# Constant matmuls on TensorE while it waits for the tokens' inverse roots, at five boundaries of a four-layer kernel

## The chip, the cores and the metric

The kernel runs on one core of one Trainium2 chip. The metric is the device time of one execution in microseconds (us). The core has five engines that run their own instruction streams and meet through semaphores: TensorE (PE, matmul), VectorE (DVE), ScalarE (ACT), GpSimd (POOL) and SyncE (SP, which here issues the loads of the weights).

## The reference

The reference is two model blocks of two layers each, run one after the other on 256 tokens of width 1024, all in float32.

```python
def first_block(x, ...):                       # l = 0, 1
    h = rmsnorm(x, g_mix[l])
    q, k, v, gates = split(h @ w_in[l])
    x = x + (g_sb * stick_breaking(q, k, v) @ w_o_sb[l] + g_fx * forgetting(q, k, v) @ w_o_fox[l]) @ w_out[l]
    h = rmsnorm(x, g_ffn[l])
    x = x + (swiglu(h, ...) if l == 0 else moe_swiglu(h, w_router, w_gu_exp, w_dn_exp))

def second_block(x, c, ctx, ...):              # l = 0, 1; a context xc of 256 tokens runs beside x in l = 0
    h = modulate(rms_norm(x, g_pre_mix[l]), sh1, sc1)
    y = mLSTM branch, grouped attention branch, neighbourhood attention branch of h @ w_in[l]
    x = x + ga1 * rms_norm(merge_branches(y) @ w_out[l], g_post_mix[l])
    f = conv_ffn(modulate(rms_norm(x, g_pre_ffn[l]), sh2, sc2), w_up[l], conv_w[l], conv_b[l], w_down[l])
    x = x + ga2 * rms_norm(f, g_post_ffn[l])
```

A norm divides each token's row by the root of its mean square. So no projection that follows a norm can start before that token's root is known, and the root needs the whole of the row that the projection before has just finished.

## The kernel before

Every projection is a *segment*: a list of *units* of weights (128 x 1024 floats each) that SP loads, ACT rounds to an upper part (`w_hi`, line 1031) and DVE to the rest (`w_lo`, line 1542). PE multiplies each unit three times: upper weights by upper activations, upper weights by lower activations, lower weights by upper activations. A segment's results lie in PSUM, which has eight banks of 128 x 512 floats. Banks 0 to 3 hold the results of the projections (4 to 7 as well in a feed-forward segment), and steps beside them (attention, transposes) use banks 4 to 7.

The order of the work is that of a list, `plan`, made once; each engine walks the list in order. Where a norm stands between two segments, the plan has a `turn` step, and the segment behind it is started by `first_pair` on PE (lines 2575 to 2626). What happens at such a boundary:

- DVE (or ACT and DVE) finishes the residual sum `x_tm` from the last PSUM result.
- ACT squares each of the two tiles of 128 tokens with a running sum (line 1430), takes the root (line 1435); DVE takes the reciprocal (line 2215) and multiplies the identity by it (line 2216). That makes one diagonal matrix for each tile of tokens.
- PE multiplies 128 x 128 blocks of `x_tm` by these diagonals (`turn_item`, line 2571). So it transposes the tokens and divides by the root at once. Each item is two float32 matmuls, and each of these appears in the trace as two pieces. Four items go ahead, in banks 4 to 7; the first needs the first root for its first half, and the second root for its other half.
- ACT and DVE turn each item into `h_hi` and `h_lo`, with the gain only (lines 1455 and 2233) in the first block, with gain and shift (lines 1448, 1459, 2223, 2236) in the second. `first_pair` then multiplies two units of weights chunk by chunk (line 2616) as the items come, with one more `turn_item` behind each chunk.

PE has nothing to do between the last matmul of the old segment and the first `turn_item`. The boundaries that the change touches are five of the eight that go through `first_pair`:

| boundary | segment whose first pair follows | where in the code | about at (us) |
|---|---|---|---|
| A | first block, layer 1, stick-breaking q and k (`s_sb`) | `first_layer`, line 639 | 459 to 463 |
| B | first block, layer 1, router (8 columns) | `first_layer`, line 693 | 687 to 692 |
| C | second block, layer 0, feed-forward, 512 tokens | `second_layer`, line 859 | 1770 to 1775 |
| D | second block, layer 1, mLSTM q (`s_mq`) | `second_layer`, line 747 | 2199 to 2209 |
| E | second block, layer 1, feed-forward, 256 tokens | `second_layer`, line 859 | 2631 to 2638 |

At D the old segment ends with results for 512 tokens in banks 0 to 3. DVE adds the first two tiles (banks 0 and 1, line 1654) and raises `o_added`; the other two tiles are added later.

Of the kernel before, what the change touches and what calls it, by code (L numbers as in the profile page):

```python
# [16 lines left out]
TT = T // P  # L17
# [30 lines left out]
AHEAD = 2  # L48
# [67 lines left out]
class Segment:  # L116
# [4 lines left out]
    def __init__(self, units, iters, mode, at, evac, A=None, B=None, N=None, tiles=None, dst=None, scale=None, bias=None,  # L121
                 M=None, tmp=None, route=None, n_branch=None, gates=None, bias_layer=None, o=None, cw=None, cb=None,
                 down=None, ex=None, half=None, buf=None, mod_rows=None, mod_places=None, dt=0, after=0, gate0=None, y_pairs=0, y_turned=0,
                 ys=None, sums=False, spare=None):
        self.units, self.iters, self.n = units, iters, len(units)

        self.paced = mode in ("fm", "tm")
        self.uses, self.ride = [], {}
        self.dt, self.after, self.gate0, self.y_pairs, self.y_turned = dt, after, gate0, y_pairs, y_turned
        self.looped = iters > 2  # L130
        assert not self.looped or self.n % RAW == 0 and self.n % HL == 0 and all(u[0] >= 0 for u in units)
        self.results = max(u[0] for u in units) + 1
        self.next, self.first = None, False
        self.alone = mode == "moe"
        self.turned = {}
        self.sig = self.unit0 = self.result0 = self.flag = self.before = self.ready = self.x_at = None
        self.ringed, self.apart, self.clear = False, 0, None
        self.routes, self.routed = False, None
        self.split_at = [sum(u[0] >= 0 for u in units[:j]) for j in range(len(units) + 1)]
        self.splits, self.mods = self.split_at[-1], len(units) - self.split_at[-1]  # L140
        self.mod_rows, self.mod_places, self.mod0 = mod_rows, mod_places, None
        self.down = down if down is not None else self.results
        self.ex, self.half, self.buf = ex, half, buf
        self.mode, self.at, self.evac = mode, at, evac
        self.A, self.B, self.N, self.tiles = A, B, N, tiles
        self.dst, self.scale, self.bias, self.M = dst, scale, bias, M
        self.tmp, self.route, self.o, self.cw, self.cb = tmp, route, o, cw, cb
        self.n_branch, self.gates, self.bias_layer = n_branch, gates, bias_layer
        self.ys = ys
        self.sums, self.spare, self.tail, self.gains, self.turn, self.late, self.early = sums, spare, None, None, None, None, AHEAD  # L150
        self.down_at = next((j for j, u in enumerate(units) if mode == "ffn" and u[0] == FB), None)

    def parts(self, j):
# [59 lines left out]
def build(nc, a, out):  # L213
    ctx = ExitStack()
    with ctx:
# [18 lines left out]
        causal = sb("causal", [P, TT, T], F32R)  # L234
        anti = sb("anti", [P, TT, T], F32R)
        ident_r = sb("ident_r", [P, P], F32R)
# [218 lines left out]
        def tm_units(w, c0, q=0, chunks=DC, width=NT):  # L455

            n = UNIT // width
            return [(q, k, min(n, chunks - k), k == 0, k + n >= chunks, width,
                     lambda it, k=k: w[k * P:min(k + n, chunks) * P, c0:c0 + width].rearrange("(c p) n -> p c n", p=P))
                    for k in range(0, chunks, n)]  # L460
# [161 lines left out]
        def first_layer(l, before, ctx_turned):  # L622
# [13 lines left out]
            else:  # L636
                done = (main.results_saved, before.result0 + before.results * before.iters)
                turn_norm([0], lambda s: g_mix, None, 0, ready=[done] * TT, parts_first=True)
            s_sb = add_segment("fm", sum((fm_units(w, QK_SB + q * 2 * P, q) for q in range(4)), []), A=H, N=T, evac="fm", dst=qk,
                               scale=[HD ** -0.5] * 2 + [1.0] * 2)  # L640
            s_vsb = add_segment("tm", tm_units(w, V_SB), A=H, tiles=TT, evac="tm", dst=v_sb)
            if l == 0:
                spread(Step("prepare", dict(count), steps=2), units_of(s_vsb)[1:3])
# [43 lines left out]
            if l % 2:  # L687
# [5 lines left out]
                router = add_segment("fm", fm_units(a["w_router"][l // 2], 0, 0, N_EXP), A=H, N=T, evac="rows", dst=logits, bias=None,  # L693
                                     M=N_EXP)
                router.routes = True
                half, used, _ = router.uses[0][0]
                add("route", logits=logits, route=route, buf=buf, ready=(half_saved[half], used + 1), src=plan[-2])
                router_step = plan[-1]
# [12 lines left out]
            n = D_FF // FE  # L711
# [8 lines left out]
        def second_layer(l, before, ctx_turned):  # L720
# [12 lines left out]
            def span(t):  # L733
# [13 lines left out]
            s_mq = add_segment("fm", sum((fm_units(w, MQ + q * 2 * P, q) for q in range(2)), []), A=H, N=nq * P, evac="fm",  # L747
                               dst=mqk[:, 0:ML_H, :], scale=[1.0] * 2)
            if nq == TT:
                s_mq.late, s_mq.early = s_mq.turned["fresh"][0], AHEAD + 2  # L750
            s_mg = add_segment("fm", fm_units(w, MG, 0, 4 * ML_H), A=H, N=2 * T, evac="rows", dst=rows[0:4 * ML_H, 0, :],
                               bias=gate_bias[0:4 * ML_H, DEPTH + l:DEPTH + l + 1], M=4 * ML_H)
# [95 lines left out]
            for k in range(2):  # L848
# [12 lines left out]
                              evac="conv", tmp=view(FREE + 4096, 4, 2 * T), o=o, cw=col_second(l, "conv_w"),  # L861
                              cb=col_second(l, "conv_b"), down=FB, spare=view(3072, 2, 512))
            seg.tail = Step("tail", dict(count), rows=mod_rows if more else None, l=l + 1)
            seg.gains = gains(1, diag, nq // TT)
            n = FB * (D_FF // FE)
            seg.clear = mixed
# [1442 lines left out]
        def _(pe):  # L2309
# [265 lines left out]
            def first_pair(seg):  # L2575
# [3 lines left out]
                ah, al = seg.A  # L2579
                if not seg.paced:  # L2580
                    pe.wait_ge(seg.sig.results_saved, seg.result(0, 0))
                total = sum(seg.units[j][2] for j in range(2))
                sides = [o for o in order if (o[0] + 1) * T <= seg.N]
                for n, (s, base, own) in enumerate(sides):
# [286 lines left out]
```

## Time and profile before

| | |
|---|---|
| median of 3 runs | 2851.9 us (2850.53 to 2852.31) |
| the profiled execution's own time | 2847.78 us |
| its span, first to last instruction | 2846.0 us |
| PE busy | 2700.3 us, 95% |
| DVE busy, ACT busy | 59%, 48% |
| mean granted clock of TensorE | 0.984 of full speed |
| chain that ended last, by engine | PE 81%, ACT 7%, DVE 7%, issue 5% |

The granted clock is the share of full speed (2.4 GHz) that the chip lets TensorE have; in this profile it is 1.00 or 0.50 (1.2 GHz) at any one time. A mean between the two says for how much of a stretch it was down. A matmul's busy time includes its way through the array, so of matmuls in a row the distance from start to start is what each one costs.

### The profile page before, as it was taken

What the parts mean: (1) busy time and instruction counts of PE and PEld (TensorE: products, weight loads), DVE (VectorE), ACT (ScalarE), POOL (GpSimd) and SP (SyncE); (2) the same over time, 40 slices, a digit from 0 to 9 for tenths busy, and PEclk for the clock granted to TensorE, in tenths of its full rate; (3) what the DMA queues carried; (4) which work ended last, traced back from release to release, by engine and by line L of the source; (5) the groups of instructions that cost most, each with busy time, mean ns of one, the idle gap of its engine ahead of it and who ended that gap; (6) DMA issues with size and microseconds to landing.
All of it is one profiled execution on the core that took longest, in us unless ns stands there. A gap on an engine that the chain in (4) does not pass through costs nothing.

```text
span 2846.0 us, 40880 instructions
## 1 busy us (share of the span) xinstructions
PE 2700.3 (95%) x14980; PEld 2167.5 (76%) x14980; DVE 1677.7 (59%) x2555; ACT 1372.7 (48%) x2229; POOL 46.4 (2%) x58
## 2 busy tenths in 40 slices
PE   8999999998999999999999999999999899989998
PEld 7668888666888888677776677777777677667987
DVE  5654445655898998354545545553454456455766
ACT  5544345654776776333335344432333434445654
POOL 1000000000000000000000100000000010010000
PEclk9999999999999999899999999999999999999999
DMA  7437895434899997322231213364452234333464
GB/s 225 128 115 224 268 297 162 127 119 168 296 324 323 326 323 266 94 67 60 78 89 49 78 56 97 115 181 126 134 179 74 82 99 124 90 104 118 144 184 141
DMA packets 352458, 444.88 MB, mean 156 GB/s; under 512 B 19616, under 2 KB 197920, under 8 KB 352288
## 3 DMA queue, kind: packets, MB, share of 16 engines
q1 hardware_dynamic: 349792, 435.44, 48.7%
q0 software_dynamic: 2208, 6.79, 0.8%
q8 instruction: 109, 1.79, 0.3%
q14 instruction: 61, 0.50, 0.1%
q10 hardware_dynamic: 288, 0.36, 0.0%
HBM read 441.48 MB, written 1.05 MB: 155 GB/s over the span
## 4 chain that ended last, share of the span: by engine, by line
PE 81%; ACT 7%; DVE 7%; issue 5%; DMA 1%; SPq 0%; ACTq 0%; DVEq 0%
PE ps L2381 21%; PE ps L2409 16%; PE ps L2368 14%; PE ps L2422 8%; PE ps L2413 4%; ACT w_hi L1031 2%; PE ps L2430 2%; PE ps L2616 2%; PE ps L2731 2%; PE ps L2714 2%; PE ps L2571 1%; PE ps L2720 1%; PE ps L2447 1%; PE ps L2751 1%; DVE att L2081 1%
## 5 line engine op out<-in xcount | busy, mean ns | idle before, releaser
L1542 DVE TENSOR_TENSOR w_lo<-raw,w_hi 128x1024 fp32r<-128x1024 f32 (+1 forms) x578 | 684.9, 1200 | 529.8 <-ACT w_hi L1031 462.1
L1031 ACT ACTIVATE w_hi<-raw 128x1024 fp32r<-128x1024 f32 (+1 forms) x578 | 587.1, 1030 | 273.4 <-PE ps L2381 126.0
L2409 PE MATMUL ps<-w_hi,h_hi 128*128 128x512 f32 (+1 forms) x992 | 402.8, 408 | 11.5 <-DVE h_lo L1993 3.9
L2409 PE MATMUL ps<-w_hi,h_lo 128*128 128x512 f32 (+1 forms) x992 | 379.4, 385 | 0.0
L2368 PE MATMUL ps<-h_hi,w_hi 128*128 128x256 f32 (+1 forms) x1008 | 301.5, 324 | 15.5 <-ACT w_hi L1031 10.3
L2422 PE MATMUL ps<-w_lo,h_hi 128*128 128x512 f32 (+1 forms) x992 | 297.6, 384 | 0.0
L2368 PE MATMUL ps<-h_lo,w_hi 128*128 128x256 f32 (+1 forms) x1008 | 296.7, 320 | 0.0
L2368 PEld LDWEIGHTS ps<-h_hi,w_hi 128*128 128x128 f32 x1008 | 192.2, 191 | 49.4 <-ACT w_hi L1031 16.7
L2409 PEld LDWEIGHTS ps<-w_hi,h_hi 128*128 128x128 f32 x992 | 187.7, 189 | 48.4 <-issue 12.7
L2422 PEld LDWEIGHTS ps<-w_lo,h_hi 128*128 128x128 f32 x992 | 183.0, 188 | 39.5
L2381 PE MATMUL ps<-w_hi,act_hi 128*128 128x512 f32 x528 | 211.6, 401 | 0.0
L2409 PEld LDWEIGHTS ps<-w_hi,h_lo 128*128 128x128 f32 x992 | 187.4, 189 | 28.9 <-issue 1.0
L2381 PE MATMUL ps<-w_hi,act_lo 128*128 128x512 f32 x528 | 209.1, 396 | 0.0
L1542 DVE TENSOR_TENSOR w_lo<-arena,w_hi 128x1024 fp32r<-128x1024 f32 (+1 forms) x192 | 201.7, 1085 | 7.9 <-ACT w_hi L1031 7.4
L2368 PEld LDWEIGHTS ps<-h_lo,w_hi 128*128 128x128 f32 x1008 | 192.4, 191 | 12.8
L1369 ACT ACTIVATE arena<-ps,att 128x512 f32<-128x512 f32 (+2 forms) x128 | 72.7, 568 | 244.0 <-DVE att L2081 160.8
L1031 ACT ACTIVATE w_hi<-arena 128x1024 fp32r<-128x1024 f32 (+1 forms) x192 | 175.2, 947 | 24.2 <-PE ps L2381 23.6
L2368 PE MATMUL ps<-h_hi,w_lo 128*128 128x256 f32 (+1 forms) x1008 | 177.2, 318 | 0.0
L2368 PEld LDWEIGHTS ps<-h_hi,w_lo 128*128 128x128 f32 x1008 | 149.8, 191 | 13.1
L2381 PE MATMUL ps<-w_lo,act_hi 128*128 128x512 f32 x528 | 152.9, 400 | 0.0
L2381 PE MATMUL ps<-w_hi,h_hi 128*128 128x512 f32 (+1 forms) x384 | 145.7, 379 | 2.8 <-issue 2.8
L2381 PE MATMUL ps<-w_hi,h_lo 128*128 128x512 f32 (+1 forms) x384 | 142.8, 372 | 0.0
(301 smaller groups left out, 4214.3 us busy)
## 6 DMA issues: line engine op xcount, KB each, us to landing
raw<-in_w_in SPq DMA_DIRECT2D x196, 512.0 KB, 3.7
arena<-in_w_mod SPq DMA_DIRECT2D x96, 512.0 KB, 5.6
raw<-in_w_up SPq DMA_DIRECT2D x88, 512.0 KB, 4.7
raw<-in_w_gu_exp SPq DMA_DIRECT2D x64, 512.0 KB, 5.6
arena<-in_w_gu_exp SPq DMA_DIRECT2D x64, 512.0 KB, 4.8
arena<-in_w_gu_exp SPq DMA_DIRECT2D x64, 384.0 KB, 4.0
arena<-in_w_dn_exp SPq DMA_DIRECT2D x48, 512.0 KB, 6.4
raw<-in_w_gu_dense SPq DMA_DIRECT2D x44, 512.0 KB, 7.4
```

Of the source, the lines that this page charges most:

```text
L1031: nc.scalar.activation(w_hi[:, half, 0:n], place[:, 0:n], ACT.Copy).then_inc(seg.sig.hi_ready, 1)
L1369: nc.scalar.activation(prob[:, i0 % 2, 0:nk], z, ACT.Exp, bias=att[:, i0 % 2:i0 % 2 + 1], accum_out=att[:, 2 + i0 % 2:3 + i0 % 2]).then_in ...
L1542: nc.vector.tensor_tensor(w_lo[:, half, 0:n], place[:, 0:n], w_hi[:, half, 0:n].bitcast(F32), ALU.subtract).then_inc(seg.sig.lo_ready, 1)
L2368: ins = mm(dst, w[:, f0:f0 + wide], x[:, k + c, 0:seg.N], start=upper and k + c == 0 and x is ah, stop=not upper and k + c == DC - 1)
L2381: ins = mm(dst, x, w[:, c * width:(c + 1) * width], start=upper and opens and c == 0 and x is xh, stop=not upper and closes and c == m - 1)
L2409: ins = mm(ps[:, 2 * h + p % 2, 0:width], x[:, k + c, p * P:(p + 1) * P], wh[:, c * width:(c + 1) * width], start=opens and c == 0 and x i ...
L2413: ins = mm(ps[0:wide, 2 * h + p % 2, 0:seg.N], wh[:, f0:f0 + wide], x[:, k + c, 0:seg.N], start=opens and c == 0 and x is ah, stop=False)
L2422: ins = mm(ps[:, 2 * h + p % 2, 0:width], ah[:, k + c, p * P:(p + 1) * P], wl[:, c * width:(c + 1) * width], start=False, stop=last and no ...
L2430: ins = mm(ps[0:wide, 2 * h + p % 2, 0:seg.N], wl[:, f0:f0 + wide], ah[:, k + c, 0:seg.N], start=False, stop=last)
L2616: ins = mm(ps[0:wide, bank, cols_], w[:, f0:f0 + wide], x[:, k + c, cols_], start=begins and kind == 0, stop=ends and kind == 2)
L2714: ins = mm(z[:, lo:hi], e["q"], e["k"][:, lo:hi], start=lo == 0, stop=not adds)
L2731: ins = nc.tensor.transpose(ps[:, bank, c * P:(c + 1) * P], prob[:, i0 % 2, c * P:(c + 1) * P], ident[:, :])
```

## The change

A segment gets a field `warm`: a bank, a count, a semaphore and a value. In `first_pair`, before anything else of the new segment, PE waits until the semaphore has that value and then issues that many matmuls of `ident_r` (the 128 x 128 identity, the stationary operand) by `causal` (128 x 512 constants), all into the same PSUM bank. Nothing reads what they write, and the bank is overwritten by a later matmul that starts its sum anew. The semaphore tells that the bank's last result has been read. Both constants have been in SBUF since the start.

```diff
@@ Segment.__init__
-        self.sums, ..., self.late, self.early = sums, spare, None, None, None, None, AHEAD
+        self.sums, ..., self.late, self.early, self.warm = sums, spare, None, None, None, None, AHEAD, None
@@ first_layer, behind add_segment of s_sb                          (boundary A)
+            if l:
+                s_sb.warm = (2, 10, mod_saved, before.at["mod"] + before.iters)
@@ first_layer, behind router.routes = True                        (boundary B)
+                half, used, _ = outs.uses[0][0]
+                router.warm = (2 * half, 10, half_saved[half], used + 1)
@@ second_layer, under "if nq == TT:" of s_mq                       (boundary D)
+                s_mq.warm = (0, 24, o_added, before.gains.at["o_added"] + 1)
@@ second_layer, behind seg.tail of the feed-forward                (boundaries C and E)
+            half, used, _ = outs.uses[1 if nq > TT else 0][0]
+            seg.warm = (2 * half, 9 if nq > TT else 20, half_saved[half], used + 1)
@@ first_pair, on PE
                 if not seg.paced:
                     pe.wait_ge(seg.sig.results_saved, seg.result(0, 0))
+                if seg.warm is not None:
+                    bank, n, saved, value = seg.warm
+                    pe.wait_ge(saved, value)
+                    for i in range(n):
+                        mm(ps[:, bank, :], ident_r[:, :], causal[:, :, :].rearrange("p t k -> p (t k)"), start=True, stop=True)
                 total = sum(seg.units[j][2] for j in range(2))
```

So there are 10 + 10 + 9 + 24 + 20 = 73 matmuls more, and five waits more on PE. No instruction of another engine is changed, and no DMA.

## Rows read from the trace of the kernel before

**Rows 1.** Waits of PE over the span: who for whom, us, times, longest.
```profile
PE ps L2571 <- DVE arena L2216: 38.0, 13, 9.3
```
**Rows 2.** Windows: stretch, length, busy (count) by engine, granted clock, DMA share, GB/s.
```profile
463.80:467.20 3.40, 3.40 (x18) 3.40 (x17) 1.94 (x4) 1.67 (x4) 0.00 (x0) 0.50 0.00 0
692.50:695.90 3.40, 3.40 (x18) 2.91 (x17) 2.01 (x5) 1.66 (x4) 0.00 (x0) 0.50 1.05 389
1774.50:1777.90 3.40, 3.07 (x15) 3.08 (x15) 1.35 (x4) 2.10 (x7) 0.00 (x0) 0.50 0.02 5
2204.60:2208.00 3.40, 0.77 (x2) 0.50 (x2) 3.16 (x7) 2.80 (x6) 0.00 (x0) 0.50 0.00 0
2208.00:2211.40 3.40, 3.07 (x15) 3.07 (x15) 1.35 (x4) 1.35 (x4) 0.00 (x0) 0.50 0.00 0
...
2638.00:2641.40 3.40, 3.40 (x15) 3.26 (x15) 1.42 (x4) 1.31 (x4) 0.00 (x0) 0.50 0.00 0
```
**Rows 3.** Timeline of PE at boundary A: start, us, instruction, count, idle before.
```profile
458.56 0.62 PE L2381 MATMUL ps<-w_lo,act_hi 128*128 128x512 f32 x2
462.20 0.46 PE L2571 MATMUL ps<-arena,x_tm 128*128 128x128 f32 x2 [3.01 <-DVE arena L2216]
463.05 2.69 PE L2571 MATMUL ps<-arena,x_tm 128*128 128x128 f32 x14 [0.39 <-DVE arena L2216]
465.39 0.77 PE L2616 MATMUL ps<-h_hi,w_hi 128*128 128x256 f32 x2
...
467.38 0.48 PE L2616 MATMUL ps<-h_hi,w_hi 128*128 128x256 f32 x2
...
468.53 0.48 PE L2616 MATMUL ps<-h_hi,w_hi 128*128 128x256 f32 x2
```
**Rows 4.** Timeline of PE at boundary B.
```profile
691.29 2.29 PE L2571 MATMUL ps<-arena,x_tm 128*128 128x128 f32 x14 [0.39 <-DVE arena L2216]
693.24 0.56 PE L2616 MATMUL ps<-h_hi,w_hi 128*8 128x256 f32 x1
...
696.07 0.36 PE L2616 MATMUL ps<-h_hi,w_hi 128*8 128x256 f32 x1
...
696.86 0.36 PE L2616 MATMUL ps<-h_hi,w_hi 128*8 128x256 f32 x1
```
**Rows 5.** Timeline of DVE and PE at boundary D.
```profile
2199.73 1.23 DVE L1654 TENSOR_TENSOR arena<-ps,arena 128x1024 f32<-128x1024 f32 x1 [1.51 <-PE ps L2381]
...
2206.66 0.77 PE L2571 MATMUL ps<-arena,x_tm 128*128 128x128 f32 x2 [6.97 <-DVE arena L2216]
...
2208.33 3.29 PE L2571 MATMUL ps<-arena,x_tm 128*128 128x128 f32 x14 [0.91 <-DVE arena L2216]
...
2210.87 0.54 DVE L2223 TENSOR_SCALAR arena<-ps,mod_gain,mod 128x256 f32<-128x256 f32 x1 [1.16 <-PE ps L2571]
```
**Rows 6.** Timeline of PE at boundaries C and E.
```profile
1773.59 0.46 PE L2571 MATMUL ps<-arena,x_tm 128*128 128x128 f32 x2 [3.15 <-DVE arena L2216]
...
1774.83 3.30 PE L2571 MATMUL ps<-arena,x_tm 128*128 128x128 f32 x14 [0.77 <-DVE arena L2216]
...
2636.68 0.77 PE L2571 MATMUL ps<-arena,x_tm 128*128 128x128 f32 x2 [5.79 <-DVE arena L2216]
```
**Rows 7.** Chain that ended last: start, us, eight 128x512 matmuls, at half and full clock.
```profile
1204.49 3.64 PE ps L2413 x8
1209.06 1.83 PE ps L2413 x8
```
**Rows 8.** Timeline of PE: two other waits, the next instruction behind each.
```profile
1405.44 1.53 PE L2522 MATMUL ps<-ident,arena 128*128 128x128 f32 x8 [2.21 <-DVE arena L1984]
...
2540.73 0.49 PE L2714 MATMUL ps<-arena 64*128 64x256 f32 x2 [3.02 <-ACT arena L1369]
```
**Rows 9.** Windows behind the waits of the group above.
```profile
1405.90:1409.30 3.40, 3.40 (x12) 2.85 (x11) 2.39 (x9) 2.17 (x8) 0.00 (x0) 0.50 0.49 149
...
2542.50:2545.90 3.40, 3.40 (x28) 2.31 (x27) 2.74 (x4) 1.19 (x4) 0.49 (x1) 1.00 0.19 27
```

More of the change, by code:

```diff
@@ L149, in __init__ @@
         self.ys = ys
-        self.sums, self.spare, self.tail, self.gains, self.turn, self.late, self.early = sums, spare, None, None, None, None, AHEAD
+        self.sums, self.spare, self.tail, self.gains, self.turn, self.late, self.early, self.warm = sums, spare, None, None, None, None, AHEAD, None
         self.down_at = next((j for j, u in enumerate(units) if mode == "ffn" and u[0] == FB), None)
```

## The prediction

> **What bounds the kernel now.** I read the list of waits of PE first. PE is busy for nearly the whole span, so its waits are the only idle time that can be had. The longest entry is the wait of `turn_item` for the diagonal made from an inverse root: 38.0 us in 13 waits, the longest 9.3 us [rows 1]. The change doesn't shorten these waits: the root is made by DVE and ACT, and neither is touched. So I looked, second, for what such a wait costs beside itself, in the windows with their granted clock. Behind each of the five boundaries there is a stretch at 0.50, in sum seven windows of 3.4 us or 23.8 us [rows 2] (the window ahead of the last repeats the fourth). Third, the timeline shows the order: at A PE stops after the matmuls that start at 458.56, is idle 3.01 us, issues two pieces, and 1.6 us after they start the clock is at half [rows 2, 3]. At half clock the steps of `first_pair` take 1.99 us (465.39 to 467.38), and at full clock 1.15 us (467.38 to 468.53) [rows 3]. It is this that the change can take away: PE does something in the wait, the clock stays up, and the real matmuls behind the wait run at full speed.
>
> **What is added, and its cover.** Eight matmuls of 128x512 take 1.83 us at full clock and 3.64 us at half [rows 7], so one costs 0.23 us or 0.46 us. Per boundary, at full clock, against the idle time of PE that is there:
> - A: 10 x 0.23 = 2.3 us in 3.01 us [rows 3]. The semaphore is that of the last modulation result, and is up long before.
> - B: 10 x 0.23 = 2.3 us in a wait of the same length as at A (the step between is the same, 0.39 us before the 14 pieces in both [rows 3, 4]).
> - C: 9 x 0.23 = 2.1 us in 3.15 us [rows 6]. The semaphore is that of the first half's result, which DVE saves while PE computes the other half.
> - D: `o_added` comes when DVE's add of 1.23 us from 199.73 (all times here less 2000) ends at 200.96; 24 x 0.23 = 5.5 us from there end at 206.5. The first pieces start at 206.66, and the 14 that matter at 208.33 [rows 5]. The margin is 0.2 us to the first, 1.8 us to the second.
> - E: 20 x 0.23 = 4.6 us in 5.79 us [rows 6]; its semaphore is that of a result saved one result earlier.
>
> So the 73 matmuls, 16.8 us of PE time, lie wholly beside waits that are there anyway: cost 0. If PE is at half clock when they start, 24 of them take 11.0 us and end at 212.0, 3.7 us too late; that is the upper end, kept for the third rival. The five waits on semaphores cost nothing either, as each is up when PE reaches it but for D's; behind it only `turn_item`s are queued, which need the roots that come 5.7 us later. No other engine waits for the added matmuls. The bank that they write is one whose reader has finished.
>
> **What is gained, term by term, if the clock stays up.**
> - A. The 14 pieces take 2.34 us at A (463.05 to 465.39). At B they take 1.95 us (691.29 to 693.24), of which 0.74 us lie behind 692.50, in the half-clock window; halved, that makes 1.58 us at full clock. Gain 2.34 - 1.58 = 0.76 us. Then one step of 1.99 us in place of 1.15 us: 0.84 us. Sum 1.6 us [rows 2 to 4]. The upper bound is half of PE's 3.40 busy us in that window, 1.7 us [rows 2].
> - B. 0.37 us in the 14 pieces, and two steps in 2.83 us (693.24 to 696.07) in place of 2 x 0.79 us: 1.25 us. Sum 1.6 us, bound 1.7 us [rows 2, 4].
> - D. Here ACT and DVE stand between the items and the first multiplication, so PE's gain counts only as far as their chain starts earlier. DVE's work on the third item starts 2.54 us after the 14 pieces do (208.33 to 210.87) [rows 5]. Ten pieces must be done for it: at half clock 10 x 3.07/14 = 2.2 us, at full clock 10 x 1.58/14 = 1.1 us. So the chain starts 1.1 us earlier. Lower end 0 (another step of ACT or DVE is late instead), upper end half of PE's busy time in both windows, (0.77 + 3.07)/2 = 1.9 us [rows 2].
> - C and E. The same 14 pieces (3.30 us at C, wholly at half clock), the same chain with DVE: 1.1 us each. Lower end 0, upper ends 3.07/2 = 1.5 us, and (0.77 + 3.40)/2 = 2.1 us, taking the window ahead as D's [rows 2, 6].
>
> All five: 1.6 + 1.6 + 1.1 + 1.1 + 1.1 = 6.5 us, between 0 and 8.9 us. Behind a boundary PE is the engine that sets the time, so an earlier start is handed on.
>
> The Trainium skill ("TensorE: Matmul & The Clock Gate", Terms) prices a throttled time at that time multiplied by the lost share. By it the seven windows would be worth 23.8/2 = 11.9 us. The rows disagree: in two of the seven windows PE was busy 0.77 of 3.40 us, and time in which PE only waits gives nothing back.
>
> **Does the clock stay up?** The rows of before say that this isn't settled by the length of one wait: behind a wait of 2.21 us the clock fell, behind one of 3.02 us it did not [rows 8, 9]. What is left of the gaps after the change:
> - A: 0.7 us and, between the roots, 0.39 us. Kept, I take 0.95.
> - B: the same: 0.9, as what follows are 8-column matmuls.
> - D: 1.3 us ahead of the added matmuls (PE has been idle since 206.66 - 6.97 = 199.69 [rows 5]), then 0.2 us and 0.91 us. Kept: 0.9.
> - C: 1.1 us and 0.77 us with only two pieces between, together nearly the gap that fell in rows 8. Kept: 0.5.
> - E: 1.2 us and then a gap between the roots of the kind that D has (0.91 us). Kept: 0.5.
>
> The likeliest outcome is that A, B and D are kept and one of C and E: 1.6 + 1.6 + 1.1 + 1.1 = 5.4 us. The profiled execution took 2847.8 us with a span of 2846.0, so this one would be 2842.4 and 2840.6. The runs' median is 2851.9 us, 4.1 us above the profiled execution. I put the forecast on the median: 2851.9 - 5.4 = 2846.5 us. The 4.1 us may be half-clock stretches that last longer in those executions. The Trainium skill says (same page, Part 1) that where the clock changes varies from run to run, and advises not to fit a count; no row here shows more than one execution.
>
> **The rivals.**
> 1. *More comes back* (chance 0.22). All five are kept, and the timed executions had longer half-clock stretches than this profile: 6.5 to 9 us, some 2844 us, and down to 2840 us by the page's price. For it: the 4.1 us. Against: two gaps at C and E.
> 2. *The change doesn't do what it says* (0.28). The clock falls all the same at most boundaries, because the rest of the gap suffices or because it was on its way down already, or it stays up there and falls some us later in the real work. Then at most A and one more are gained, 0 to 3 us: about 2850.5 us. For it: clock falls at gaps of 2.21 us [rows 8, 9]. Against: at A and B the added work leaves under 1 us.
> 3. *Slower* (0.05). PE is already at half clock when the added matmuls start, which needs the clock to fall in the 1.3 us ahead of them at D or in the tail of the old segment elsewhere. They then take 0.46 us each: D ends 3.7 us late, E (9.2 us from 2636.68 - 5.79 = 2630.9 to 2640.1, where its second root is there at about 2638.0) 2.1 us late, and the real work is at half clock as before. 2851.9 + 5.8 = 2857.7 us. It decides from the point where 24 matmuls take longer than the 7.4 us from 200.96 to 208.33, that is where more than 8 of them run at half clock. Against: at A, B, C and E the added matmuls follow the old segment's last one without a pause.
>
> **How the numbers follow.** Forecast case 0.45, with its own range of 2844.5 to 2848.5 us. A measurement of this kernel can tell about 0.2%, or 5.7 us, from no change. The forecast lies just inside it; about 0.2 of its 0.45 lie beyond, with all 0.22 of rival 1: faster 0.42. The rest of it and rival 2: same 0.53. Rival 3: slower 0.05. The range of 2842 to 2852 us leaves out rival 3, the far end of rival 1 and little else.
>
> **What would show it.** In the profile after, 73 matmuls of `causal` by `ident_r` in the five waits, 0.23 us apart; the granted clock 1.00 from the wait on at A, B and D; the 14 pieces at 1.6 us where they took 2.3 to 3.4 us; the first multiplication at D about 2.0 us behind the pieces' start. The wait for DVE's diagonal shrinks by 16 us in the list while the time falls by a third of that. I am wrong if the 14 pieces still take over 3 us at D, if the added matmuls are 0.46 us apart, or if the pieces are fast and the span isn't shorter, which would mean that ACT and DVE, not PE, set the steps behind the boundary.

## The result and the profile after

By the medians the kernel went from 2849.91 us (19 runs, 2846.62 to 2855.56) to 2845.17 us (19 runs, 2836.67 to 2849.74). The ratio to the kernel before is 0.998, with a 95% interval of 0.9973 to 0.9987, so 3.7 to 7.7 us were gained. The profiled execution took 2843.1 us with a span of 2841.3 us, against 2847.8 and 2846.0 us before: 4.7 us less. The prediction gave 0.53 to "same", which it took to reach up to 5.7 us from no change, and 0.42 to "faster". By the medians "same" came; but with 19 runs each the interval ends 3.7 us short of no change, so the kernel did get faster.

The first two lines of the page and the list of PE's waits (engine, line and tile, for whom, us in total, times, longest), of the kernel after:

```profile
span 2841.3 us, 41028 instructions
PE 2712.5 (95%) x15053; PEld 2175.9 (77%) x15053; DVE 1676.6 (59%) x2555; ACT 1372.3 (48%) x2229; POOL 47.5 (2%) x58
```
```profile
PE ps L2578 <- DVE arena L2223: 20.5, 13, 9.0
```

The wait for the diagonal is the one of [rows 1]; its lines are 7 further down in the new file. It fell from 38.0 to 20.5 us, that is by 17.5 us, and the span by 4.7 us: the list counts the added matmuls as work, so it says nothing of what was gained. What the matmuls took shows in the list of the added instructions by tile (durations least/median/largest in ns, first and last start):

```profile
L2593 PE MATMUL ps<-causal,ident_r x73: 387/389/496, 458.7 to 2630.4; 128*128 128x512 f32 x73
```

All 73 are there. The granted clock of the kernel after, by windows (the columns of [rows 2]):

```profile
463.80:467.20 3.40, 3.40 (x32) 3.40 (x31) 2.26 (x5) 2.02 (x5) 0.00 (x0) 1.00 0.00 0
1779.80:1783.20 3.40, 3.40 (x18) 3.40 (x17) 0.71 (x3) 0.71 (x3) 0.00 (x0) 0.51 0.00 0
2204.10:2208.00 3.90, 3.55 (x27) 3.29 (x28) 2.92 (x6) 2.81 (x9) 0.00 (x0) 1.00 0.01 2
2633.20:2636.60 3.40, 3.33 (x15) 3.27 (x15) 1.35 (x4) 1.28 (x3) 0.00 (x0) 0.50 0.00 0
```

At A the same stretch held 18 matmuls at 0.50 and now holds 32 at 1.00. At D the clock is full too. At E it is still half, and there is a stretch at half clock behind C, in a place where the trace of before has none. The timelines say what each of these is worth.

**A and B.** PE of the kernel after (start, us, instruction, count, idle before and its releaser):

```profile
458.70 2.43 PE L2593 MATMUL ps<-causal,ident_r 128*128 128x512 f32 x10
461.87 0.46 PE L2578 MATMUL ps<-arena,x_tm 128*128 128x128 f32 x2 [0.74 <-DVE arena L2223]
462.72 1.83 PE L2578 MATMUL ps<-arena,x_tm 128*128 128x128 f32 x14 [0.39 <-DVE arena L2223]
464.30 0.48 PE L2628 MATMUL ps<-h_hi,w_hi 128*128 128x256 f32 x2
...
466.63 0.48 PE L2628 MATMUL ps<-h_hi,w_hi 128*128 128x256 f32 x2
...
689.56 1.83 PE L2578 MATMUL ps<-arena,x_tm 128*128 128x128 f32 x14 [0.39 <-DVE arena L2223]
...
693.54 0.36 PE L2628 MATMUL ps<-h_hi,w_hi 128*8 128x256 f32 x1
```

From the start of the 14 pieces to the third group of real multiplications it is 466.63 - 462.72 = 3.91 us at A, against 468.53 - 463.05 = 5.48 us in [rows 3]. At B to the fourth group it is 3.98 us against 5.57 us in [rows 4]. Both gave 1.6 us. The 14 pieces cost 464.30 - 462.72 = 1.58 us from start to start, the figure of the prediction.

**D.** The same view, with two instructions of ACT and DVE, from the added matmuls of D on:

```profile
2196.82 5.75 PE L2593 MATMUL ps<-causal,ident_r 128*128 128x512 f32 x24 [1.32 <-DVE arena L1661]
2202.48 0.46 PE L2578 MATMUL ps<-arena,x_tm 128*128 128x128 f32 x2
2204.15 1.83 PE L2578 MATMUL ps<-arena,x_tm 128*128 128x128 f32 x14 [1.21 <-DVE arena L2223]
2205.12 0.56 ACT L1455 ACTIVATE arena<-ps,mod,mod_gain 128x256 f32<-128x256 f32 x1 [1.79 <-PE ps L2578]
2205.57 0.54 DVE L2230 TENSOR_SCALAR arena<-ps,mod_gain,mod 128x256 f32<-128x256 f32 x1 [0.35 <-PE ps L2578]
2206.28 0.47 PE L2628 MATMUL ps<-h_hi,w_hi 128*128 128x256 f32 x2 [0.30 <-ACT h_hi L1466]
...
2211.70 0.48 PE L2628 MATMUL ps<-h_hi,w_hi 128*128 128x256 f32 x2
```

And in the kernel before, what answers to that ACT instruction and to the last two groups:

```profile
2210.01 0.56 ACT L1448 ACTIVATE arena<-ps,mod,mod_gain 128x256 f32<-128x256 f32 x1 [2.50 <-PE ps L2571]
...
2211.34 0.52 PE L2616 MATMUL ps<-h_hi,w_hi 128*128 128x256 f32 x2
...
2216.59 0.48 PE L2616 MATMUL ps<-h_hi,w_hi 128*128 128x256 f32 x2
```

The 24 lie in the wait without gaps, and the pieces are fast. The first multiplication comes 2.13 us behind the pieces' start, where it took 2211.34 - 2208.33 = 3.01 us before, and the fifth group 7.55 us, where it took 8.26 us. So 0.9 us came in at first, and 0.7 us were handed on. DVE's work on the third item starts 1.42 us behind the pieces, where it took 2.54 us in [rows 5]: 1.12 us earlier, as forecast. ACT's work on the second item starts 0.97 us behind them, where it took 2210.01 - 2208.33 = 1.68 us: only 0.71 us earlier. PE's first multiplication now waits 0.30 us for what ACT makes of it, and ACT's lead of 0.7 us is what is left five groups on.

**C.** The kernel after:

```profile
1765.71 2.24 PE L2593 MATMUL ps<-causal,ident_r 128*128 128x512 f32 x9
1769.03 0.46 PE L2578 MATMUL ps<-arena,x_tm 128*128 128x128 f32 x2 [1.07 <-DVE arena L2223]
1770.26 1.83 PE L2578 MATMUL ps<-arena,x_tm 128*128 128x128 f32 x14 [0.77 <-DVE arena L2223]
...
1777.30 0.39 PE L2628 MATMUL ps<-h_lo,w_hi 128*128 128x256 f32 x1 [0.65 <-DVE h_lo L2243]
...
1778.92 0.39 PE L2628 MATMUL ps<-h_hi,w_hi 128*128 128x256 f32 x1 [0.77 <-ACT h_hi L1466]
...
1783.37 0.61 PE L2578 MATMUL ps<-arena,x_tm 128*128 128x128 f32 x4
```

The instructions of before that answer to the last two:

```profile
1784.47 0.39 PE L2616 MATMUL ps<-h_hi,w_hi 128*128 128x256 f32 x1 [0.77 <-ACT h_hi L1459]
...
1787.43 0.61 PE L2571 MATMUL ps<-arena,x_tm 128*128 128x128 f32 x4
```

The pieces took 3.30 us in [rows 6] and now take 1.83 us. But from their start to the four pieces at the end it is 13.11 us, against 1787.43 - 1774.83 = 12.60 us before: 0.5 us lost. The pieces' gain is there and is handed on: the multiplication behind the second pause comes 8.66 us behind the pieces' start, where it took 1784.47 - 1774.83 = 9.64 us, so 1.0 us earlier. Both traces have the two pauses of PE, one made by DVE and one by ACT. Of the two traces only that of after has a fall of the clock behind them, for 3.4 us, and it costs 1.5 us. In that stretch there are only multiplications without a wait, so all of it counts. Before, the half-clock stretch lay on the pieces, where ACT and DVE set part of the time; the change moved it to a place where PE sets all of it.

**E.** The kernel after:

```profile
2626.02 4.74 PE L2593 MATMUL ps<-causal,ident_r 128*128 128x512 f32 x20
2631.97 0.46 PE L2578 MATMUL ps<-arena,x_tm 128*128 128x128 f32 x2 [1.22 <-DVE arena L2223]
2633.27 3.36 PE L2578 MATMUL ps<-arena,x_tm 128*128 128x128 f32 x14 [0.84 <-DVE arena L2223]
2636.28 0.50 PE L2628 MATMUL ps<-h_hi,w_hi 128*128 128x256 f32 x1
```

The clock falls at the end of the second of the two gaps that are left, 1.22 and 0.84 us, and the multiplication comes 3.01 us behind the pieces' start, as before. E gave nothing in this execution.

**The sum over the whole span.** DVE's instructions are the same in both kernels, so the time between two of them can be compared from trace to trace, and the whole span can be cut into such differences. Negative is earlier than in the trace of before:

| stretch | after | e1 | e2 | e3 | e4 | e5 | e6 | e7 | e8 | e9 | e10 | e11 |
|---|---|---|---|---|---|---|---|---|---|---|---|---|
| A | -1.6 | -1.6 | 0 | -0.1 | -1.6 | -1.6 | -1.6 | -1.6 | -1.6 | -1.6 | -1.6 | -1.6 |
| B | -1.6 | -1.6 | 0 | 0 | -1.6 | -1.6 | -1.6 | -1.6 | -1.6 | -1.6 | -1.6 | -1.6 |
| C | +0.5 | +1.3 | +0.5 | 0 | -0.1 | +0.5 | +0.5 | +0.5 | +0.5 | -1.0 | -0.2 | -1.0 |
| D | -0.7 | +0.4 | -0.7 | 0 | -0.7 | -0.7 | -0.7 | -0.7 | +3.1 | -0.7 | -0.7 | -0.7 |
| E | 0 | +0.7 | 0 | 0 | -1.0 | -1.0 | -0.1 | -1.0 | -0.1 | -1.0 | -0.1 | -1.0 |
| whole span | -4.7 | +1.8 | +0.7 | -0.5 | -3.6 | -2.6 | -8.1 | -8.8 | -1.5 | -2.3 | -2.0 | -3.8 |

The five boundaries of the change sum up to -3.4 us. The other 1.3 us are outside them, nearly all in three places: 2.4 and 1.0 us less in two stretches (226 to 262 us and 699 to 725 us) and 2.3 us more ahead of 100 us. In the first and the last of these a stretch at half clock is there in one trace and not in the other, in the second it lies 2 us elsewhere in the work. The first and the last lie ahead of the first added matmul at 458.7 us, so they can't come of the change. So one pair of traces can't price the change as a whole (e1 gains at A and B and its profiled execution is 1.8 us longer than that of before), but it can price a boundary: A, B and D read alike in every trace with the same edit.

Without any matmuls C, D and E vary too. e1 has none there and reads +1.3, +0.4 and +0.7: at D and E its clock is down for 10.2 us, where it was 6.8 us in before, and at C it falls twice, on the pieces and again behind the two pauses:

```profile
1773.80:1777.20 3.40, 3.40 (x17) 3.20 (x16) 2.33 (x5) 2.31 (x6) 0.00 (x0) 0.50 0.00 0
1784.00:1787.40 3.40, 3.40 (x19) 3.40 (x18) 0.45 (x2) 0.32 (x2) 0.00 (x0) 0.51 0.00 0
```

Before, e3 and e10, also without matmuls at C, have one fall there, on the pieces, and read 0, 0 and -0.2.

### The profile page after: what moved, and what is told of

Its sections match the earlier page's. It is cut to its first block, busy times and chain, and to the rows that moved or that the text cites. A ratio compares the mean times of both kernels' runs of the same rounds, so it can differ in the third digit from the quotient of the medians.

```text
span 2841.3 us, 41028 instructions
## 1 busy us (share of the span) xinstructions
PE 2712.5 (95%) x15053; PEld 2175.9 (77%) x15053; DVE 1676.6 (59%) x2555; ACT 1372.3 (48%) x2229; POOL 47.5 (2%) x58
## 4 chain that ended last, share of the span: by engine, by line
PE 82%; ACT 7%; DVE 7%; issue 5%; DMA 0%; ACTq 0%; DVEq 0%
PE ps L2388 22%; PE ps L2416 16%; PE ps L2375 14%; PE ps L2429 8%; PE ps L2420 4%; ACT w_hi L1038 2%; PE ps L2437 2%; PE ps L2628 2%; PE ps L2743 2%; PE ps L2726 2%; PE ps L2732 1%; PE ps L2578 1%; PE ps L2454 1%; PE ps L2763 1%; PE ps L2332 1%
```

## The experiments

Times are medians; the ratio is to the runs of the kernel before on the same chip, with its 95% interval. e1 to e4, e5 to e8, and e9 to e11 ran together, each set on one chip.

**e1_first_block: A and B alone.**
```diff
-                s_mq.warm = (0, 24, o_added, before.gains.at["o_added"] + 1)
-            half, used, _ = outs.uses[1 if nq > TT else 0][0]
-            seg.warm = (2 * half, 9 if nq > TT else 20, half_saved[half], used + 1)
```


> The added matmuls of boundaries A and B alone (20 of the 73). Theory (the clock stays up and the real work behind the wait runs at full speed): A gives 1.6 us and B 1.4 us, as the two profiles put it, so 3 us faster than before, and nearly the whole of the measured 4.7 us of the five. The 14 pieces take 1.8 us at both. Rival (each boundary gives its 1.1 to 1.6 us, whatever stands behind it): 3 us of 6.5, with the rest in the other half. Rival (the gain is chance, in where the clock falls elsewhere): anything within 2 us of before.

2847.38 us against 2851.71 us, ratio 0.9989 (0.9979 to 0.9999), that is 3.1 us less (0.3 to 6.0) by the ratio and 4.3 us by the medians. The 3.2 us of A and B lie within this wide interval. At D the clock falls ahead of the pieces as in before, and they take 3.35 us.

**e2_second_block: C, D and E alone.**
```diff
-                s_sb.warm = (2, 10, mod_saved, before.at["mod"] + before.iters)
-                router.warm = (2 * half, 10, half_saved[half], used + 1)
```


> The added matmuls of boundaries C, D and E alone (53 of the 73). Theory (D keeps its clock and gives 0.5 to 1 us; C only moves the fall of the clock into the matmuls some us later and gives nothing; E falls between its two roots and gives nothing): 0.5 to 1.5 us faster than before. Rival (each of the three gives 1.1 us as forecast): 3.3 us faster. Rival (C costs more than it gives, as its half-clock stretch lands where PE has no pause): 0 to 1 us slower.

2848.29 us, ratio 0.9986 (0.9975 to 0.9998), that is 4.0 us less (0.6 to 7.1). Its trace accounts for 0.2 us at the three boundaries, and for 1.2 us where E is kept, as e4 and e9 show it can be. The interval leaves room for the second of these; its middle isn't explained.

**e3_waits_only: the five waits without the matmuls.**
```diff
-                    for i in range(n):
-                        mm(ps[:, bank, :], ident_r[:, :], causal[:, :, :].rearrange("p t k -> p (t k)"), start=True, stop=True)
```


> The five new waits of PE on semaphores, and none of the 73 matmuls. Theory: all that helps is the matmuls, so this is before within 0.5 us, half-clock stretches behind all five boundaries included. Rival (the waits themselves shift PE's work against the others and bring some of the gain): 1 us or more faster. Rival (a wait costs): 0.1 us each, 0.5 us slower.

2853.61 us, ratio 1.001 (1.0001 to 1.002). No boundary differs from before by more than 0.1 us in its trace, and the wait for the diagonal is whole again:
```profile
PE ps L2578 <- DVE arena L2223: 38.1, 14, 9.0
```
So the matmuls, not the waits, make the gain. The 1.9 us on the slow side by the medians is more than the 0.5 us of the second rival, and the trace has no place for it. The mean granted clock of these runs is a little lower than that of before's (0.982 against 0.983 in the median), so half-clock stretches elsewhere may have made it; it stays open.

**e4_narrow: the same matmuls with 16 of the identity's 128 columns.**
```diff
-                        mm(ps[:, bank, :], ident_r[:, :], causal[:, :, :].rearrange("p t k -> p (t k)"), start=True, stop=True)
+                        mm(ps[0:16, bank, :], ident_r[:, 0:16], causal[:, :, :].rearrange("p t k -> p (t k)"), start=True, stop=True)
```


> The same 73 matmuls of 512 columns, at the same places, with 16 columns of the identity as stationary operand in place of 128, so that they write 16 partitions of the bank: PE is as long busy, an eighth of the array works. Theory A (it counts that PE is issuing matmuls): as the change, 4.7 us faster than before. Theory B (it counts how much of the array works): the clock falls behind all five boundaries as in the kernel before, and time is before's within 1 us. In both profiles the clock fell once behind 16-column matmuls that PE had issued without a pause (at 2262 and 2258 us), which speaks for B.

2845.48 us, ratio 0.9975 (0.9965 to 0.9984). The added instructions of this kernel by tile:
```profile
L2593 PEld LDWEIGHTS ps<-causal,ident_r x73: 92/94/98, 457.2 to 2632.3; 128*16 128x16 f32 x73
L2593 PE MATMUL ps<-causal,ident_r x73: 389/396/401, 457.4 to 2632.5; 128*16 128x512 f32 x73
```
Their weight loads take half the time (94 against 188 ns), the matmuls nearly the same (396 against 389 ns). A, B and D came out as with the full ones, with the clock at 1.00. E was kept in this execution, with the same 20 matmuls that did not keep it in that of after. At C the clock fell on the pieces (-0.1), as in before, where all eight other traces with matmuls there kept it through them; one trace can't say whether the narrow ones hold it less well at that place.

The expectation took the fall near 2260 us as evidence on 16-column matmuls. What stands ahead of it are matmuls with 4 columns of weights in 16 rows (`16*4`), in this kernel:
```profile
2254.08 3.59 PE L2509 MATMUL ps<-arena,ident 16*4 16x512 f32 x8 [0.88 <-DVE arena L1941]
```
PE issues eight of them without a pause behind a wait of 0.88 us, and in all thirteen traces the clock falls during them or behind them. So the result of e4 is one for 128 rows by 16 columns at four places in one execution, and must not be carried to anything smaller.

**e5_filled: waits filled up to the root, and 2 to 5 matmuls between the two roots.**
```diff
-                s_sb.warm = (2, 10, mod_saved, before.at["mod"] + before.iters)
+                s_sb.warm = (2, 12, mod_saved, before.at["mod"] + before.iters, 2)
...
-            seg.warm = (2 * half, 9 if nq > TT else 20, half_saved[half], used + 1)
+            seg.warm = (2 * half, 13 if nq > TT else 25, half_saved[half], used + 1, 4)
@@ turn_item(st, i, between), in the loop over the two tiles
+                    if t and between:
+                        for k in range(between[1]):
+                            mm(ps[:, between[0], :], ident_r[:, :], causal..., start=True, stop=True)
```


> The change with the rest of each wait filled as well: 12, 12, 13 and 25 added matmuls ahead of the first root at A, B, C and E (10, 10, 9 and 20 in the change), and 2, 2, 4, 5 and 4 more between the first and the second root at A to E. Theory (E lost its clock in what was left of its gap): E now keeps it, the 14 pieces take 1.8 us there and it gives the 1.0 us that it gave in the run with narrow matmuls; C's pieces were fast already, and its later fall comes from pauses behind them, so C gives nothing more. So 1 us faster than the change, 5.7 us faster than before. Rival (the filling runs past the roots): the pieces start late, up to 0.5 us at each boundary, and the time is the change's or 1 us above it.

2844.13 us, ratio 0.9974 (0.9961 to 0.9986). PE of this kernel at E:
```profile
2629.06 5.87 PE L2596 MATMUL ps<-causal,ident_r 128*128 128x512 f32 x25
2635.02 0.46 PE L2581 MATMUL ps<-arena,x_tm 128*128 128x128 f32 x2
2635.24 1.17 PE L2578 MATMUL ps<-causal,ident_r 128*128 128x512 f32 x4
2636.32 1.83 PE L2581 MATMUL ps<-arena,x_tm 128*128 128x128 f32 x14
```
No gap is left and the pieces take 1.83 us. E gave 1.0 us, here and in e7 and e11, the three kernels that fill it. With 20 and the gaps left, E was kept in two traces of seven (e4 and e9, not after, e2, e6, e8, e10). Three of three against two of seven can still be chance. At C the same filling changed nothing (+0.5): the pieces had been fast before it, and the two pauses behind them were still there.

**e6_more_places: the change, and matmuls in four more waits.** These are ahead of layer 0's feed-forward of the first block, ahead of the first mLSTM segment of the second block, and two in the routing.
```diff
+            seg.warm = (2 * half, 10, half_saved[half], used + 1)          # layer 0 feed-forward
+                s_mq.warm = (0, 10, constants_set, 1)                      # second block, layer 0
+                    for i in range(11):                                    # routing; 5 more behind the gathers
+                        mm(ps[:, 4, :], ident_r[:, :], causal..., start=True, stop=True)
```


> The change, and added matmuls in four more waits: 10 ahead of the feed-forward of layer 0 of the first block, 11 while PE waits for the router's choice and 5 behind the first gather of the experts' tokens, and 10 at the start of layer 0 of the second block, where both profiles have 10.2 us at half clock. Theory: the first gives 0.8 to 2.4 us (what this boundary differed by between the profiles so far), the router's 1 to 1.6 us, the last 1.6 to 3 us: 4 us faster than the change, 8 to 9 us faster than before. Rival (the waits there are made of several short ones, and the clock falls in the next one): under 1.5 us faster than the change.

2840.67 us (6 runs), ratio 0.9964 (0.9952 to 0.9976). In the routing the clock is 1.00 over the whole in this trace, where before had 0.72:
```profile
700.00:712.00 12.00, 9.96 (x58) 8.44 (x57) 9.15 (x18) 5.90 (x7) 0.00 (x0) 1.00 0.39 115
```
Its 1.0 us is there in the trace of after too, though, without the edit. Layer 0's feed-forward has 2.4 us less than before, but so have after, e1 and e3, with nothing added there. So these traces don't show what of e6's 8.1 us is the edit's; its median is 4.5 us below the change's, over another set of runs.

**e7_both: e5 and e6 together.**


> The two edits together: filled waits, and the four more places. Theory: their gains add, as each is another half-clock stretch: 5 us faster than the change, 10 us faster than before. Rival (a gain at one place only moves the next fall): as the better of the two alone.

2841.56 us, ratio 0.9971 (0.9961 to 0.9981). E's 1.0 us came on top in the profile, but the median isn't better than e6's. At the start of the second block PE shows what the third rival of the prediction was about:
```profile
1136.96 4.64 PE L2600 MATMUL ps<-causal,ident_r 128*128 128x512 f32 x10 [2.32 <-issue]
```
Ten added matmuls behind a gap of 2.32 us run at half clock, 0.46 us each, and take 4.64 us in place of 2.4 us. From 1120 to 1161 us the trace is 0.7 us shorter than before all the same, so no cost of them shows.

**e8_overrun: 48 matmuls at D in place of 24.**
```diff
-                s_mq.warm = (0, 24, o_added, before.gains.at["o_added"] + 1)
+                s_mq.warm = (0, 48, o_added, before.gains.at["o_added"] + 1)
```


> The change with 48 matmuls in place of 24 at D. Theory (the cover at D is the 7.3 us from the semaphore to the second root): 48 x 0.23 = 11.0 us from 2196.8 end at 2207.8, where the second root is there at 2204.1, so 3.7 us later than the change, 1 us faster than before. Rival (PE's start isn't what the steps behind wait for, as ACT and DVE set them): under 2 us later than the change.

2847.63 us, ratio 0.9991 (0.9982 to 1.0). PE at D:
```profile
2196.66 11.17 PE L2593 MATMUL ps<-causal,ident_r 128*128 128x512 f32 x48 [1.31 <-DVE arena L1661]
2207.67 1.95 PE L2578 MATMUL ps<-arena,x_tm 128*128 128x128 f32 x16
2209.92 0.36 PE L2628 MATMUL ps<-h_hi,w_hi 128*128 128x256 f32 x1 [0.30 <-ACT h_hi L1466]
```
The first multiplication comes 2209.92 - 2196.66 = 13.26 us behind the start of the added matmuls, where the kernel after has 2206.28 - 2196.82 = 9.46 us: 3.8 us later. By the cover of the prediction, 24 x 0.23 = 5.5 us more would go into the 1.8 us that were left there: 3.7 us. So the cover was read rightly, and beyond it each matmul costs its whole time. The median is 2.5 us above the change's, from another set of runs.

**e9_pauses_at_c: the change, with the two pauses behind C's pieces filled.**
```diff
@@ first_pair, feed-forward with two sides, n == 0, j == 0, ahead of chunk 4 kind 1 and chunk 6 kind 0
+                                    if kind:
+                                        last_h, last_n, _ = st.seg.uses[1][1]
+                                        pe.wait_ge(half_saved[last_h], last_n + 1)
+                                    for i in range(2 if kind else 3):
+                                        mm(ps[:, 3, :], ident_r[:, :], causal..., start=True, stop=True)
```


> The change, and at C five more matmuls inside the first pair: two before the multiplication that waits 0.65 us for h_lo of its fifth chunk, three before the one that waits 0.77 us for h_hi of its seventh, into a bank read before. Theory (at C the clock is kept through the root's wait and lost in these pauses, and then the half-clock stretch lies on matmuls that PE sets the pace of): no fall at C, and C gives 1.0 us against before, where it costs 0.5 us in each of the profiles with the change's nine. So 1.5 us faster than the change. Rival (the fall at C comes from the root's wait, late): still a fall at 1780 us and C costs 0.5 us.

2844.53 us, ratio 0.9982 (0.9974 to 0.9991). PE of this kernel behind C:
```profile
1771.90 1.83 PE L2578 MATMUL ps<-arena,x_tm 128*128 128x128 f32 x14 [0.77 <-DVE arena L2223]
...
1778.13 0.63 PE L2623 MATMUL ps<-causal,ident_r 128*128 128x512 f32 x2
...
1779.65 0.86 PE L2623 MATMUL ps<-causal,ident_r 128*128 128x512 f32 x3
...
1783.51 0.61 PE L2578 MATMUL ps<-arena,x_tm 128*128 128x128 f32 x4
```
```profile
1780.90:1784.30 3.40, 3.33 (x28) 3.27 (x28) 1.36 (x7) 1.26 (x3) 0.00 (x0) 1.00 0.00 0
```
There is no stretch at half clock, and from the pieces to the four at the end it is 1783.51 - 1771.90 = 11.61 us, 1.0 us less than before and 1.5 us less than after. Five matmuls in two pauses of under 0.8 us turned C's sign. The medians of e9 and of the change (2844.53 and 2845.17 us) don't tell 1.5 us apart.

**e10_without_c: the change without C.**
```diff
-            seg.warm = (2 * half, 9 if nq > TT else 20, half_saved[half], used + 1)
+            seg.warm = None if nq > TT else (2 * half, 9 if nq > TT else 20, half_saved[half], used + 1)
```


> The change without the nine matmuls of C. Theory: C's are worth minus 0.5 us, so this is 0.5 us faster than the change; its clock falls at C before the 14 pieces, as in the kernel before. Rival (the clock then falls at other places as chance has it): C as before, and no more can be told.

2845.68 us, ratio 0.9984 (0.9975 to 0.9994). C stands at -0.2 in its trace, with the fall on the pieces again:
```profile
1775.19 2.76 PE L2578 MATMUL ps<-arena,x_tm 128*128 128x128 f32 x14 [0.77 <-DVE arena L2223]
```
By the traces C as the change has it (+0.5, six times) is 1.5 us worse than filled. It is 0.5 to 0.7 us worse than with no matmuls in e3 and here (0 and -0.2), and 0.8 us better than with none in e1 (+1.3). So it isn't shown that the nine cost anything against none. The medians of e9 and e10 don't tell the two apart, as differences of 1 us can't be told.

**e11_best: e7 with e9's edit, and at the second block's start 5 + 4 matmuls around the last scatter in place of 10 behind it.**


> All that helped: filled waits at the five boundaries, the pauses at C, the feed-forward of layer 0, the router; and at the start of layer 0 of the second block five matmuls in the 1.4 us ahead of the last scatter and four behind it, in place of ten behind the branch, which ran at half clock there (10 in 4.6 us) and gave 0.5 us. Theory (the clock has to be kept before the pause, not recovered in it): the 6.8 to 10.2 us at half clock there go, worth 1.5 to 3 us, and C's 1.5 us: 3 us faster than the kernel with both edits, 12 us faster than before. Rival (the 2.3 us that PE needs behind the branch lose the clock whatever is ahead): 1.5 us faster than that kernel.

2839.58 us (7 runs), ratio 0.997 (0.9958 to 0.9982). C, D and E are all kept (-1.0, -0.7, -1.0). The start of the second block didn't gain; ACT's and DVE's weights stop PE there, between matmuls that were not filled, and then the clock falls:
```profile
1143.28 0.80 PE L2639 MATMUL ps<-h_hi,w_lo 128*128 128x256 f32 x2 [1.95 <-DVE w_lo L1551]
```
Of all kernels it has the lowest median. By the intervals it can't be told from e6 (0.9964) or e7 (0.9971), and the change was timed in another set of runs (0.998, 0.9973 to 0.9987), with an interval that overlaps with all three. That the three are better than the change is likely and not shown.

## Why the prediction was right, and where not

**The forecast.** 2846.5 us were forecast and 2845.17 us measured; 5.4 us were to be gained, and 4.7 us came by the medians, 5.7 us by the ratio. Part of that agreement is luck. The 19 runs of before have a median of 2849.91 us, 2.0 us under the one that the forecast started from. And the boundaries gave 3.4 us in the profiled execution: 1.1 us less than forecast because neither C nor E was gained, 0.5 us because C cost, 0.4 us because D gave less. The rest of its 4.7 us came in places where nothing was edited.

**The cover: right.** "Cost 0" for 16.8 us of added PE time held at all five: in none does the first or the 14 pieces' start come later against DVE's work than in before. The 24 at D ran 0.23 us apart and e8 found the edge of the cover where the working put it. The third rival's condition, half clock when the added work starts, held at none of the five; e7 shows it at another place.

**A and B: right in mechanism and size.** 1.6 us each, with nothing between the pieces and the multiplications but PE. The chances of 0.95 and 0.9 were if anything low: the ten traces with these two edits have them all.

**D: right in mechanism, too large in size.** The step with ten pieces (2.2 us at half clock, 1.1 us at full) let DVE's chain start 1.1 us earlier, and it did, by 1.12 us. What the sum left out is ACT's work on the second item, which came only 0.71 us earlier. It is what the first multiplication now waits for: 0.9 us came there, and 0.7 us five groups on. The lower end of the range had named this ("another step of ACT or DVE is late instead").

**C: wrong.** "An earlier start is handed on" held: 1.0 us of the pieces' gain were still there 8.7 us on. The step that failed is that only the windows the change would remove were priced, and nothing for a fall that comes in their place. The clock was kept through the pieces, as the 0.5 allowed, but 7 to 9 us behind their start are pauses of 0.65 and 0.77 us that DVE and ACT make, and the half-clock stretch came behind these, where it costs 1.5 us. So the gain was +1.1 us in the forecast and measured -0.5 us, and with the pauses filled (e9, e11) it is 1.0 us. In before, e3, e4 and e10, which had their fall on the pieces, none came behind the pauses; in e1 one came there as well, so an earlier fall doesn't rule it out. The second rival named this way ("it stays up there and falls some us later in the real work") and priced it as no gain, not as a loss.

**E: as the 0.5 said.** Lost in five of the seven traces with this edit, that of after among them, kept in two, and kept in all three that leave no gap. Of the five that kept it, four also have the stretch at half clock near 2535 us that is told of at the end, and e7 alone kept it without; so that the filling did it is likely and not shown. Kept, it gives 1.0 us, where 1.1 was forecast.

**From the profiled execution to the median.** I put the difference of 4.1 us between them down to half-clock stretches, as a guess. With 19 runs the difference is 2.1 us. The runs bear the guess out: of the 81 runs of before that went with the experiments, the six with a mean granted clock of 0.980 took 2854.0 us on average, the 23 with 0.984 took 2848.0 us, and the six with 0.986 took 2845.1 us. The traces have half-clock stretches in PE-bound work that come and go without any edit there (one of 3.4 us at 517 us in e3 and e4 alone, others at 634 or 1596 us in some), and one of them is worth 1.6 us, as at A; the one near 2535 us is worth 2.5 us. The 35 runs of before that went with e1 to e4 spread from 2842.8 to 2858.5 us. The Trainium skill ("TensorE: Matmul & The Clock Gate", Part 1) says that where the clock rises at the start of matmul work varies from run to run. The traces agree, and show it for the falls too: the one at 517 us is in two of thirteen.

The Trainium skill's price of a throttled time (same page, Terms) made 11.9 us of the seven windows. Of those seven, six are gone or moved in the trace of after, and they gave 3.4 us; filled out, in e11, A to E give 5.9 us. The measurement decides: a half-clock stretch is worth half of it only where PE alone sets the time, as at A and B (1.6 of 3.4 us), and 0.7 to 1.0 us where ACT and DVE stand between (D's is 6.8 us long).

**The sign in the list of waits.** The prediction said: "The wait for DVE's diagonal shrinks by 16 us in the list while the time falls by a third of that". It was 17.5 us and 4.7 us, a good quarter.

## What to carry to other kernels

Where TensorE must wait for other engines ahead of work that it alone sets, independent matmuls into an unread bank kept its clock: at A, B and D in every trace that has them. They are free up to the moment at which the awaited result comes. So count them from the semaphore that frees the bank to that moment, and fill a gap between two results as well, which at E was kept three times of three filled and two of seven open. Look at what follows too: a run of small pauses some microseconds behind can take the clock all the same, and then in dearer work. Fill those as well. Judge such an edit by the time between two instructions of another engine in both traces, at each place, and in several traces, because half-clock stretches elsewhere come and go by 1.6 to 2.5 us each, and the very place that is edited varies without the edit (C by 1.5 us).

## What the runs showed that I had not expected

- Matmuls with 16 columns of weights held the clock at four of the five boundaries in one execution (e4: A, B, D and E, not C), at half the time of a weight load.
- Pauses of 0.65 and 0.77 us within 2 us of each other were followed by 3.4 us at half clock, in all six traces in which the pieces of C had been kept by added matmuls and the pauses were open (after, e2, e5 to e8), and in e1. In the two with five matmuls in them (e9, e11) no fall came.
- The same 20 matmuls with the same gaps of 1.22 and 0.84 us at E kept the clock in e9 and not in after. Both traces that kept it so (e4, e9) have a further stretch at half clock some 90 us ahead (granted 0.60 and 0.57 in 2535 to 2543 us), and the five that did not have none; which of the two brings the other about, if either, wasn't tried. This stretch is in e1, e5 and e11 as well. It begins in the wait of 3.02 us of [rows 8], of which the prediction said that the clock did not fall behind it, as in e4:
```profile
2535.49 2.08 PE L2726 MATMUL ps<-arena 64*128 64x256 f32 x8 [2.78 <-ACT arena L1376]
```
The eight matmuls behind it take 2.08 us here and 1.13 us in before. In five of thirteen traces the clock falls in that one wait, and in eight it doesn't, so a single trace doesn't tell whether a wait loses the clock.
